# FFN up projection: one 512-column matmul for the high weight half times both activation halves

## The chip, the cores and the metric

The kernel runs on one core of a Trainium2 chip. The metric is the device time of that core for one launch, in microseconds. Before the change it is 1241.15 us, the median of three runs (1241.06 to 1241.66).

## The reference, cut to what matters

The program is one layer of a streaming encoder on 256 tokens of width 2048: token mixers with one combined input projection, a cross-attention, and a gated FFN with a causal depthwise convolution of three taps over the tokens. The change touches the FFN alone:

```python
D_MODEL, SEQ, D_FF, FFN_CONV = 2048, 256, 5632, 3

def conv_ffn(u, w_up, conv_w, conv_b, w_down):
    hdn = causal_dwconv(u @ w_up, conv_w, conv_b)
    g, val = jnp.split(hdn, 2, axis=-1)
    return (jax.nn.silu(g) * val) @ w_down

    h = h + conv_ffn(rmsnorm(h, norm_ffn[l]), ffn_w_up[l], ffn_conv_w[l], ffn_conv_b[l], ffn_w_down[l])
```

Everything is float32, so w_up is 2048 x 11264 and w_down is 5632 x 2048.

## The kernel before, in words

**Precision by halves.** TensorE works on the type float32r here. Each float32 operand is split into a high half (its value in float32r) and a low half (the rest). A product is the sum of three matmuls into the same PSUM columns: high weight by high activation, high weight by low activation, low weight by high activation. `three` (L1243 to L1251) issues them: L1249, L1250 and L1251 with the weight tile as the stationary operand and 256 tokens moving, L1246 to L1248 with the activations stationary and 512 weight columns moving. Each matmul instruction has its own weight load (LDWEIGHTS, on the row of PEld).

**Chunks.** All weights come in chunks of 128 x 2048 (1 MB) through a ring of three slots. SyncE (`load`, L236) fetches chunk n into `raw` when the low half of chunk n-3 is made. ScalarE (`split`, L368 to L374) waits for the landing and for the products of chunk n-3 and copies `raw` to `hi`. VectorE (`split`, L731 to L738) subtracts and writes `lo`, which lets TensorE start on the chunk and SyncE refill `raw`.

**The activations.** They stand in SBUF in transposed form as `uh` (high) and `ul` (low), two tiles of 128 x 16 x 256.

**The FFN.** It is a loop over 11 groups. A group has 12 chunks: 8 of w_up, each of them one tile of 128 hidden features (gate and value tiles in turn, c = 0 to 7), then 4 of w_down (c = 8 to 11). An up tile is `tile_product` (L1253): for each of 16 slices k of the input width, three matmuls of 256 columns into the first 256 columns of bank c % 2, so 48 matmuls. Each of the four down chunks is `row_product` (L1266) with 24 matmuls of 512 columns, 96 in all.

**Around an up tile.** PE may start tile c when its `lo` is ready and when tile c-2 has been read out of the bank (semaphore `fconv_raw`, L1686). VectorE reads it: L1193 multiplies the bank by `hf_scale` (the token's norm factor) into `craw`. ScalarE applies the first tap with the bias (`first_tap`, L685 to L694), VectorE the other two (`filter_rest`, L1168 to L1180, each instruction followed by a wait for its own end: `go`, L727). On each value tile ScalarE applies silu to the gate (L697), VectorE forms the product (L1180), ScalarE makes its high half (L683) and VectorE the low half (`gated_lo`, L1207). The down products of c = 8 and 9 take k = 0 to 2 first (36 matmuls) and then wait for the last low half.

**Order on the engines.** It is written out by hand. ScalarE, per c: split of chunk c+2, then first tap of tile c-1; at c = 8 the first tap of tile 7 and the high half of the last product come ahead of the split. VectorE, per c: `gated_lo` (c = 3, 5, 7, and 8 after the rest of the filter), split of chunk c+2, read-out of tile c, the other two taps of tile c-1; in c = 9 to 11 it adds the down products to the residual (L1111). The first group is special: tile 0 and tile 1 are computed in pieces while the last activations are still being made, and `hf_scale` is copied out of bank 3 (L1159) just ahead of the first read-out.

Of the kernel before, what the change touches and what calls it, by code (L numbers as in the profile page):

```python
# [19 lines left out]
P = 128  # L20
T = 256
# [70 lines left out]
def products(n):  # L92

    extra = {N_U: 3, N_U + 1: 3, N_U + 2: 6, N_U + 3: 1}
    return n + 1 + sum(v for m, v in extra.items() if m <= n)
# [25 lines left out]
def encoder(nc, x, mem, positions, norm_mix, w_in, mla_q_norm, mla_w_uq, mla_kv_norm, mla_w_ukv, mla_out_norm,  # L121
# [4 lines left out]
    with ctx:  # L126
        def sb(name, shape, dt=F32):
            return ctx.enter_context(nc.sbuf_tensor(name, shape, dt))
# [9 lines left out]
        raw = sb("raw", [P, RING, CH])  # L138
        hi = sb("hi", [P, RING, CH], F32R)
        lo = sb("lo", [P, RING, CH], F32R)  # L140
        uh = sb("uh", [P, KD, T], F32R)
        ul = sb("ul", [P, KD, T], F32R)
        ch = sb("ch", [P, 6, T], F32R)
        cl = sb("cl", [P, 6, T], F32R)
        tab = sb("tab", [P, C_ALL])
# [62 lines left out]
        sil, prod = at(12288, T), at(12544, T)  # L208
        gfin = at(13568, D)
        hf_diag, hf_scale = at(12800, TT, P), at(15616, T)  # L210


        s_ss, s_var, s_std, s_r, s_t = 0, 2, 4, 6, 8
# [151 lines left out]
        def _(act):  # L365
# [311 lines left out]
            def ffn_group(i, last=False):  # L677
                def at_turn(v, per):
                    return i * per + v

                def gated_hi(k):
                    act.wait_ge(S("prod_ready").sem, at_turn(k + 1 + 4, 4))
                    a.mark(act.copy(ch[:, k, :], prod[:, :]), S("gated_hi"))  # L683

                def first_tap(c):  # L685

                    s, v, k = c % 4, c % 2, c // 2
                    act.wait_ge(S("fconv_raw").sem, at_turn(c + 3, 8))

                    act.wait_ge(S("prod_ready").sem, at_turn(k + 3, 4))  # L690
                    tile = at_turn(v * FT + k, 4)
                    a.mark(act.activation(cacc[:, s, :], craw[:, s, :], ACT.Identity,  # L692
                                          scale=vecs[:, bass.ds(tile + (V_FW + 2 * 2 * FT), 1)],
                                          bias=vecs[:, bass.ds(tile + V_FB, 1)]), S("fconv_first"))  # L694
                    if v == 1:
                        act.wait_ge(S("fconv_done").sem, at_turn(2 * k + 1, 8))
                        a.mark(act.activation(sil[:, :], cacc[:, s - 1, :], ACT.Silu), S("silu_ready"))  # L697
                    elif k > 0:
                        gated_hi(k - 1)

                for c in range(GROUP):
                    if c == 8:
                        first_tap(7)
                        gated_hi(3)
                    if not (last and c >= GROUP - 2):
                        split(N_FFN + c + 2, i, GROUP)
                    if 0 < c < 8:
                        first_tap(c - 1)
# [14 lines left out]
        def _(dve):  # L723
# [440 lines left out]
            def ffn_group(i, first=False, last=False):  # L1164
                def at_turn(v, per):
                    return i * per + v

                def filter_rest(c):  # L1168

                    s, v, k = c % 4, c % 2, c // 2  # L1170
                    dve.wait_ge(S("fconv_first").sem, at_turn(c + 1, 8))
                    d.settle()
                    for tap in (1, 2):
                        col = at_turn(v * FT + k + (V_FW + (2 - tap) * 2 * FT), 4)
                        go(dve.scalar_tensor_tensor(out=cacc[:, s, tap:T], in0=craw[:, s, 0:T - tap], scalar=vecs[:, bass.ds(col, 1)],  # L1175
                                                    in1=cacc[:, s, tap:T], op0=ALU.mult, op1=ALU.add),
                           S("fconv_done") if tap == 2 else None)
                    if v == 1:
                        dve.wait_ge(S("silu_ready").sem, at_turn(k + 1, 4))
                        go(dve.tensor_tensor(prod[:, :], sil[:, :], cacc[:, s, :], ALU.mult), S("prod_ready"))  # L1180

                for c in range(GROUP):
                    n = N_FFN + c
                    if c == 8:
                        filter_rest(7)
                        gated_lo(3, at_turn)
                    if c in (3, 5, 7):
                        gated_lo((c - 3) // 2, at_turn)
                    if not (last and c >= GROUP - 2) and not (first and c == 0):
                        split(n + 2, i, GROUP)  # L1190
                    if c < 8:
                        dve.wait_ge(S("products_done").sem, at_turn(products(n), GROUP))
                        d.mark(dve.tensor_tensor(craw[:, c % 4, :], bank[c % 2][:, 0:T], hf_scale, ALU.mult), S("fconv_raw"))  # L1193
                    if 0 < c < 8:
                        filter_rest(c - 1)
                    if c >= 9:
                        for cb in ((c - 9,) if c < 11 else (2, 3)):
                            dve.wait_ge(S("products_done").sem, at_turn(products(N_FFN + 8 + cb), GROUP))
                            for t in range(TT):
                                add_bank(FFN_BANKS[cb] + t, t, cb, S("ffn_added"))  # L1200
                            if last:
                                d.settle()
                                for t in range(TT):
                                    cols = slice(cb * 512, (cb + 1) * 512)
                                    d.mark(dve.tensor_tensor(hwork[:, t, cols], hres[:, t, cols], gfin[:, cols], ALU.mult), step)

            def gated_lo(k, at_turn):  # L1207
# [1 line left out]
                d.mark(dve.tensor_tensor(cl[:, k, :], prod[:, :], ch[:, k, :].bitcast(F32), ALU.subtract), S("gated_lo"))  # L1209

            per = {S("lo_ready"): GROUP, S("fconv_done"): 8, S("prod_ready"): 4, S("gated_lo"): 4, S("ffn_added"): 8,
                   S("fconv_raw"): 8, step: 8}
            start = {s: s.n for s in per}
            start[S("prod_ready")], start[S("fconv_raw")] = 4, 2
            for s in per:
# [20 lines left out]
        def _(pe):  # L1236
# [16 lines left out]
            def tile_product(n, b, cols=P, mid=None, lo_signal=None, ks=(0, KD)):  # L1253

                s = n % RING
                for k in range(*ks):
                    if k == KD // 2 and mid:
                        mid()
                    if lo_signal and k % 2 == 0:
                        pe.wait_ge(S(lo_signal).sem, k + 2)  # L1260
                    last = three(bank[b][0:cols, 0:T], hi[:, s, k * P:k * P + cols], lo[:, s, k * P:k * P + cols],
                                 uh[:, k, :], ul[:, k, :], k == 0, k == KD - 1)
                if ks[1] == KD:
                    last.then_inc(done, 1)

            def row_product(n, xh, xl, k0, b0, start, stop, signal=True, ks=range(4), mid=None):  # L1266

# [397 lines left out]
            def ffn_group(i, first=False):  # L1665
                for c in range(8):
                    n = N_FFN + c
                    if first and c == 0:

                        ready(N_FFN)  # L1670
                        pe.wait_ge(S("hf_lo").sem, 8)
                        tile_product(N_FFN, 0, ks=(0, 8))
                        turn_hf(3)
                        pe.wait_ge(S("hf_lo").sem, 12)
                        tile_product(N_FFN, 0, ks=(8, 12))
                        ready(N_FFN + 1)
                        tile_product(N_FFN + 1, 1, ks=(0, 12))
                        pe.wait_ge(S("hf_lo").sem, 16)
                        tile_product(N_FFN, 0, ks=(12, KD))
                        spread_scale("hf", hf_diag, 3)  # L1680
                        tile_product(N_FFN + 1, 1, ks=(12, KD))
                    if first and c < 2:
                        continue
                    ready(n, i, GROUP)

                    pe.wait_ge(S("fconv_raw").sem, i * 8 + (c + 1))  # L1686
                    tile_product(n, c % 2)
                for c in (8, 9):
                    pe.wait_ge(S("gated_lo").sem, i * 4 + 3)
                    ready(N_FFN + c, i, GROUP)  # L1690
                    row_product(N_FFN + c, ch, cl, 0, FFN_BANKS[c - 8], True, False, signal=False, ks=range(3))
                pe.wait_ge(S("gated_lo").sem, i * 4 + 4)
                for c in (8, 9):
                    row_product(N_FFN + c, ch, cl, 0, FFN_BANKS[c - 8], False, True, ks=range(3, 4))
                for c in (10, 11):
                    ready(N_FFN + c, i, GROUP)
                    if c == 11:
                        pe.wait_ge(S("ffn_added").sem, i * 8 + 2)
                    row_product(N_FFN + c, ch, cl, 0, FFN_BANKS[c - 8], True, True)
# [74 lines left out]
```

## Time and profile before

| what | value |
|---|---|
| median of three runs | 1241.15 us |
| span of the profiled execution, first to last instruction | 1237.7 us |
| own time of the profiled execution | not given apart; the span and the 3.45 us up to the median are what is known |
| TensorE busy (matmuls) | 1207.8 us, 98% |
| VectorE busy | 849.8 us, 69% |
| ScalarE busy | 624.7 us, 50% |
| DMA queue of the weights | 216.31 MB, 59.9% of 16 engines |
| FFN, from the first matmul of tile 0 to the last of the last down product | 476.3 to 1224.6 us |

Busy time of matmuls is not a measure of the pace: a matmul of 256 columns shows as 283 ns, yet the next one starts 120 ns later, since they are pipelined. So the pace of TensorE is read from the starts of matmuls in the timeline, or from the length of a stretch that holds a known number of them. PEclk is the granted clock as a share of full speed.

### The profile page before, as it was taken

To read this page: it belongs to the slowest core of one execution; us is meant where nothing else is said; L and a number is where in the kernel's file an instruction comes from. 1 tells how busy PE (TensorE), PEld (TensorE's weight loads), DVE (VectorE), ACT (ScalarE), POOL (GpSimd) and SP (SyncE) were. 2 spreads that over 40 slices of the span, in tenths; PEclk is the share of its full clock that TensorE was granted. 3 is DMA by queue.
4 is the path that set the end of the run, shared out by engine and by line. 5 is a ranking of instruction groups with operands and counts; after the bars stand their busy time and mean duration, and the time that the engine had idled before them with its cause. 6 is when DMAs were issued, how large, how long until landed. Compare 5 with 4: busy or idle time off the path is not lost.

```text
span 1237.7 us, 21481 instructions
## 1 busy us (share of the span) xinstructions
PE 1207.8 (98%) x8428; PEld 1123.8 (91%) x8428; DVE 849.8 (69%) x1155; ACT 624.7 (50%) x778; POOL 0.2 (0%) x4
## 2 busy tenths in 40 slices
PE   6999999999999999999999999999999999999995
PEld 6899999988888979989898999999898989999994
DVE  6754888777376667766767667667667676676675
ACT  5545664475554557445454544454454545454444
POOL 0000000000000000000000000000000000000000
PEclk9999999999899999999999999999999999999998
DMA  9766756432655445676656757575766667575741
GB/s 274 238 160 169 197 142 171 128 104 68 219 189 170 140 153 166 193 200 183 192 171 184 194 163 203 169 208 179 193 192 179 176 188 198 152 203 168 215 156 68
DMA packets 309933, 217.09 MB, mean 175 GB/s; under 512 B 11414, under 2 KB 272254, under 8 KB 309246
## 3 DMA queue, kind: packets, MB, share of 16 engines
q1 hardware_dynamic: 309710, 216.31, 59.9%
q8 instruction: 32, 0.52, 0.2%
q10 hardware_dynamic: 176, 0.14, 0.1%
q14 instruction: 15, 0.12, 0.0%
HBM read 214.33 MB, written 2.10 MB: 175 GB/s over the span
## 4 chain that ended last, share of the span: by engine, by line
PE 92%; ACT 3%; DVE 2%; DMA 1%; SPq 1%; issue 1%; ACTq 0%; DVEq 0%
PE bank L1249 19%; PE bank L1251 19%; PE bank L1250 19%; PE bank L1246 10%; PE bank L1248 10%; PE bank L1247 10%; PE bank L1345 1%; DVE lo L738 1%; ACT hi L374 1%; PE bank L1376 1%; DMA raw<-in_cross_wkv_dram 1%; PE bank L1317 1%; PE bank L1294 1%; PE bank L1303 1%; PE bank L1355 0%
## 5 line engine op out<-in xcount | busy, mean ns | idle before, releaser
L1249 PE MATMUL bank<-uh,hi 128*128 128x256 f32 (+1 forms) x2000 | 569.9, 285 | 3.5 <-DVE lo L738 3.0
L1250 PE MATMUL bank<-ul,hi 128*128 128x256 f32 (+1 forms) x2000 | 566.4, 283 | 0.0
L1251 PE MATMUL bank<-uh,lo 128*128 128x256 f32 (+1 forms) x2000 | 566.3, 283 | 0.0
L738 DVE TENSOR_TENSOR lo<-raw,hi 128x2048 fp32r<-128x2048 f32 x196 | 448.9, 2290 | 168.0 <-ACT hi L374 166.0
L374 ACT CAST hi<-raw 128x2048 fp32r<-128x2048 f32 x196 | 372.7, 1907 | 347.3 <-PE bank L1251 224.9
L1249 PEld LDWEIGHTS bank<-uh,hi 128*128 128x128 f32 (+1 forms) x2000 | 383.5, 192 | 7.8 <-DVE lo L738 3.2
L1250 PEld LDWEIGHTS bank<-ul,hi 128*128 128x128 f32 (+1 forms) x2000 | 383.7, 192 | 0.5
L1251 PEld LDWEIGHTS bank<-uh,lo 128*128 128x128 f32 (+1 forms) x2000 | 383.5, 192 | 0.0
L1246 PE MATMUL bank<-hi,ch 128*128 128x512 f32 x472 | 185.7, 393 | 1.7 <-DVE cl L1134 1.4
L1247 PE MATMUL bank<-lo,ch 128*128 128x512 f32 x472 | 184.4, 391 | 0.0
L1248 PE MATMUL bank<-hi,cl 128*128 128x512 f32 x472 | 184.3, 390 | 0.0
L1246 PEld LDWEIGHTS bank<-hi,ch 128*128 128x128 f32 x472 | 89.4, 189 | 20.3 <-DVE cl L1134 1.8
L1248 PEld LDWEIGHTS bank<-hi,cl 128*128 128x128 f32 x472 | 89.2, 189 | 18.7
L1247 PEld LDWEIGHTS bank<-lo,ch 128*128 128x128 f32 x472 | 89.4, 189 | 17.8
L1175 DVE SCALAR_TENSOR_TENSOR arena<-arena,vecs 128x255 f32<-128x255 f32 (+1 forms) x176 | 85.2, 484 | 24.6 <-DVE arena L1175 2.3
L1193 DVE TENSOR_TENSOR arena<-bank,arena 128x256 f32<-128x256 f32 x88 | 37.3, 424 | 88.3 <-PE bank L1251 88.1
L692 ACT ACTIVATE arena<-arena,vecs 128x256 f32<-128x256 f32 x88 | 52.7, 599 | 40.4 <-DVE arena L1193 40.3
L1111 DVE TENSOR_TENSOR arena<-arena,bank 128x512 f32<-128x512 f32 x96 | 60.7, 681 | 0.9 <-PE bank L1248 0.9
L774 DVE SCALAR_TENSOR_TENSOR ul<-bank,vecs,uh 128x256 fp32r<-128x256 f32 x64 | 26.6, 477 | 16.2 <-ACT uh L404 16.1
L459 ACT COPY arena<-bank 128x256 f32<-128x256 f32 x22 | 8.2, 371 | 57.9 <-PE bank L1251 57.9
L1209 DVE TENSOR_TENSOR cl<-arena,ch 128x256 fp32r<-128x256 f32 x44 | 18.7, 426 | 27.2 <-ACT ch L683 27.2
L404 ACT ACTIVATE uh<-bank,vecs 128x256 fp32r<-128x256 f32 x64 | 25.6, 472 | 19.5 <-PE bank L1303 14.2
(212 smaller groups left out, 780.0 us busy)
## 6 DMA issues: line engine op xcount, KB each, us to landing
raw<-in_ffn_w_up_dram SPq DMA_DIRECT2D x88, 1024.0 KB, 5.8
raw<-in_ffn_w_down_dram SPq DMA_DIRECT2D x44, 1024.0 KB, 5.1
raw<-in_w_in_dram SPq DMA_DIRECT2D x28, 1024.0 KB, 5.7
raw<-in_w_out_dram SPq DMA_DIRECT2D x16, 1024.0 KB, 5.1
raw<-in_cross_wkv_dram SPq DMA_DIRECT2D x7, 1024.0 KB, 9.2
arena<-in_x_dram SPq DMA_DIRECT2D x4, 1024.0 KB, 5.9
raw<-in_cross_wq_dram SPq DMA_DIRECT2D x4, 1024.0 KB, 5.5
raw<-in_cross_wo_dram SPq DMA_DIRECT2D x4, 1024.0 KB, 5.1
```

The lines of the kernel that those rows point to most:

```text
L374: a.mark(act.copy(hi[:, n % RING, :], raw[:, n % RING, :]), S("hi_ready"))
L692: a.mark(act.activation(cacc[:, s, :], craw[:, s, :], ACT.Identity, scale=vecs[:, bass.ds(tile + (V_FW + 2 * 2 * FT), 1)], bias=vecs[:, ba ...
L738: d.mark(dve.tensor_tensor(lo[:, n % RING, :], raw[:, n % RING, :], hi[:, n % RING, :].bitcast(F32), ALU.subtract), S("lo_ready"))
L1111: d.mark(dve.tensor_tensor(hres[:, t, cb * 512:(cb + 1) * 512], hres[:, t, cb * 512:(cb + 1) * 512], bank[b][:, :], ALU.add), signal)
L1175: go(dve.scalar_tensor_tensor(out=cacc[:, s, tap:T], in0=craw[:, s, 0:T - tap], scalar=vecs[:, bass.ds(col, 1)], in1=cacc[:, s, tap:T], op ...
L1193: d.mark(dve.tensor_tensor(craw[:, c % 4, :], bank[c % 2][:, 0:T], hf_scale, ALU.mult), S("fconv_raw"))
L1246: pe.matmul(dst, xh, wh, start=start, stop=False)
L1247: pe.matmul(dst, xh, wl, start=False, stop=False)
L1248: return pe.matmul(dst, xl, wh, start=False, stop=stop)
L1249: pe.matmul(dst, wh, xh, start=start, stop=False)
L1250: pe.matmul(dst, wh, xl, start=False, stop=False)
L1251: return pe.matmul(dst, wl, xh, start=False, stop=stop)
```

## The change

`uh` and `ul` become the two halves of one tile `ux`, so that for each k the high and the low activations stand side by side, 512 columns in a row. A new `wide_product` takes the place of `tile_product` for the up tiles: per k one matmul of 512 columns (high weight by both halves, into the whole bank) and one of 256 columns (low weight by the high half, into the first 256). The two halves of the bank are added when it is read out: ScalarE copies columns 256 to 511 to SBUF (`low_half`, new instruction, with its own semaphore), VectorE adds this to columns 0 to 255, waits for its own end, and multiplies by `hf_scale` from SBUF. The order of ScalarE gets `low_half(c - 1)` ahead of the split of c+2.

```diff
-        uh = sb("uh", [P, KD, T], F32R)
-        ul = sb("ul", [P, KD, T], F32R)
+        ux = sb("ux", [P, KD, 2, T], F32R)
+        uh, ul = ux[:, :, 0, :], ux[:, :, 1, :]
...
+        up_low = at(13056, T)
...
+                def low_half(c):
+
+                    act.wait_ge(S("products_done").sem, at_turn(products(N_FFN + c), GROUP))
+                    a.mark(act.copy(up_low, bank[c % 2][:, T:2 * T]), S("up_low_taken"))
+
                 for c in range(GROUP):
+                    if 0 < c <= 8:
+                        low_half(c - 1)
                     if c == 8:
                         first_tap(7)
                         gated_hi(3)
...
                     if c < 8:
-                        dve.wait_ge(S("products_done").sem, at_turn(products(n), GROUP))
-                        d.mark(dve.tensor_tensor(craw[:, c % 4, :], bank[c % 2][:, 0:T], hf_scale, ALU.mult), S("fconv_raw"))
+                        dve.wait_ge(S("up_low_taken").sem, at_turn(c + 1, 8))
+                        go(dve.tensor_tensor(craw[:, c % 4, :], bank[c % 2][:, 0:T], up_low, ALU.add))
+                        d.mark(dve.tensor_tensor(craw[:, c % 4, :], craw[:, c % 4, :], hf_scale, ALU.mult), S("fconv_raw"))
...
+            def wide_product(n, b, ks=(0, KD)):
+
+                s = n % RING
+                for k in range(*ks):
+                    wh, wl = hi[:, s, k * P:(k + 1) * P], lo[:, s, k * P:(k + 1) * P]
+                    both_ = ux[:, k, :, :].rearrange("p a b -> p (a b)")
+                    if k < KD - 1:
+                        pe.matmul(bank[b][:, :], wh, both_, start=(k == 0), stop=False)
+                        pe.matmul(bank[b][:, 0:T], wl, uh[:, k, :], start=False, stop=False)
+                    else:
+                        pe.matmul(bank[b][:, 0:T], wl, uh[:, k, :], start=False, stop=False)
+                        pe.matmul(bank[b][:, :], wh, both_, start=False, stop=True).then_inc(done, 1)
```

In `ffn_group` of TensorE every `tile_product` of an up tile becomes a `wide_product` with the same slices.

## Rows read from the trace of the kernel before

**Rows 1.** The page: busy time and instructions of each engine.

```profile
PE 1207.8 (98%) x8428; PEld 1123.8 (91%) x8428; DVE 849.8 (69%) x1155; ACT 624.7 (50%) x778; POOL 0.2 (0%) x4
```

**Rows 2.** Who waited for whom, TensorE alone: waited for, us, times, longest.

```profile
PE bank L1249 <- DVE lo L738: 3.0, 1, 3.0
...
PE bank L1249 <- DVE arena L1193: 0.3, 1, 0.3
```

**Rows 3.** Two windows, 96 down and 384 up matmuls: us, busy per engine, PEclk, DMA.

```profile
795.71:817.50 21.79, 21.79 (x99) 18.03 (x97) 15.51 (x17) 10.16 (x8) 0.00 (x0) 1.00 0.63 180
817.50:863.57 46.07, 46.07 (x386) 46.07 (x384) 30.88 (x36) 21.95 (x22) 0.00 (x0) 1.00 0.64 188
```

**Rows 4.** Timeline of TensorE at both changes of width: start us, duration us.

```profile
795.71 0.40 PE L1246 MATMUL bank<-hi,ch 128*128 128x512 f32 x1
795.94 0.40 PE L1247 MATMUL bank<-lo,ch 128*128 128x512 f32 x1
796.18 0.39 PE L1248 MATMUL bank<-hi,cl 128*128 128x512 f32 x1
...
797.10 0.39 PE L1246 MATMUL bank<-hi,ch 128*128 128x512 f32 x1
...
817.27 0.39 PE L1248 MATMUL bank<-hi,cl 128*128 128x512 f32 x1
817.50 0.28 PE L1249 MATMUL bank<-uh,hi 128*128 128x256 f32 x1
817.61 0.28 PE L1250 MATMUL bank<-ul,hi 128*128 128x256 f32 x1
```

**Rows 5.** The page, costliest groups: a ScalarE copy out of a bank, 256 columns.

```profile
L459 ACT COPY arena<-bank 128x256 f32<-128x256 f32 x22 | 8.2, 371 | 57.9 <-PE bank L1251 57.9
```

**Rows 6.** Timeline of VectorE, tiles 2 to 4 of a steady group.

```profile
834.97 0.42 DVE L1193 TENSOR_TENSOR arena<-bank,arena 128x256 f32<-128x256 f32 x1 [1.53 <-PE bank L1251]
835.54 1.11 DVE L1175 SCALAR_TENSOR_TENSOR arena<-arena,vecs 128x255 f32<-128x255 f32 x2
836.77 0.42 DVE L1180 TENSOR_TENSOR arena<-arena 128x256 f32<-128x256 f32 x1
837.77 0.42 DVE L1209 TENSOR_TENSOR cl<-arena,ch 128x256 fp32r<-128x256 f32 x1 [0.57 <-ACT ch L683]
838.12 2.29 DVE L738 TENSOR_TENSOR lo<-raw,hi 128x2048 fp32r<-128x2048 f32 x1
840.73 0.42 DVE L1193 TENSOR_TENSOR arena<-bank,arena 128x256 f32<-128x256 f32 x1 [0.33 <-PE bank L1251]
```

**Rows 7.** Timelines after tile 7 of that group: first down matmul, then VectorE.

```profile
863.57 0.40 PE L1246 MATMUL bank<-hi,ch 128*128 128x512 f32 x1
...
863.77 0.42 DVE L1193 TENSOR_TENSOR arena<-bank,arena 128x256 f32<-128x256 f32 x1 [0.33 <-PE bank L1251]
...
867.89 0.43 DVE L1209 TENSOR_TENSOR cl<-arena,ch 128x256 fp32r<-128x256 f32 x1 [0.54 <-ACT ch L683]
869.64 2.29 DVE L738 TENSOR_TENSOR lo<-raw,hi 128x2048 fp32r<-128x2048 f32 x1 [1.32 <-ACT hi L374]
```

**Rows 8.** Timelines of the first group: VectorE copy and read-out, then tile 2.

```profile
488.41 0.42 DVE L1159 COPY arena<-bank 128x256 f32<-128x256 f32 x1
489.07 0.42 DVE L1193 TENSOR_TENSOR arena<-bank,arena 128x256 f32<-128x256 f32 x1 [0.24 <-DVE arena L1159]
...
489.64 0.36 PE L1249 MATMUL bank<-uh,hi 128*128 128x256 f32 x1 [0.31 <-DVE arena L1193]
```

**Rows 9.** The page, DMA issues: median us from issue to landing.

```profile
raw<-in_ffn_w_up_dram SPq DMA_DIRECT2D x88, 1024.0 KB, 5.8
```

More of the change, by code:

```diff
@@ L1211, in _ @@
             per = {S("lo_ready"): GROUP, S("fconv_done"): 8, S("prod_ready"): 4, S("gated_lo"): 4, S("ffn_added"): 8,
-                   S("fconv_raw"): 8, step: 8}
+                   S("fconv_raw"): 8, step: 16}
             start = {s: s.n for s in per}
@@ L1671, in ffn_group @@
                         pe.wait_ge(S("hf_lo").sem, 8)
-                        tile_product(N_FFN, 0, ks=(0, 8))
+                        wide_product(N_FFN, 0, ks=(0, 8))
                         turn_hf(3)
                         pe.wait_ge(S("hf_lo").sem, 12)
-                        tile_product(N_FFN, 0, ks=(8, 12))
+                        wide_product(N_FFN, 0, ks=(8, 12))
                         ready(N_FFN + 1)
-                        tile_product(N_FFN + 1, 1, ks=(0, 12))
+                        wide_product(N_FFN + 1, 1, ks=(0, 12))
                         pe.wait_ge(S("hf_lo").sem, 16)
-                        tile_product(N_FFN, 0, ks=(12, KD))
+                        wide_product(N_FFN, 0, ks=(12, KD))
                         spread_scale("hf", hf_diag, 3)
-                        tile_product(N_FFN + 1, 1, ks=(12, KD))
+                        wide_product(N_FFN + 1, 1, ks=(12, KD))
                     if first and c < 2:
@@ L1686, in ffn_group @@
                     pe.wait_ge(S("fconv_raw").sem, i * 8 + (c + 1))
-                    tile_product(n, c % 2)
+                    wide_product(n, c % 2)
                 for c in (8, 9):
```

## The prediction, made before the changed kernel was run

> **What bounds the kernel now.** I read the page first: TensorE is busy for 98% of the span, VectorE for 69%, ScalarE for 50% [rows 1]. That share alone can mislead, because matmuls overlap, so I looked next at who made TensorE wait. From the FFN there are two entries at most, 3.0 us once and 0.3 us once [rows 2], and the second of them is in the first group [rows 8]. In the ten groups after that TensorE never waits. So the FFN lasts as long as its matmuls take to issue, and what counts is the distance from one start to the next.
>
> The two windows give that distance. They are cut at starts of matmuls, and the code says how many lie between: 384 matmuls of 256 columns in 46.07 us, 0.1200 us each, and 96 of 512 columns in 21.79 us, 0.2270 us each, both at granted clock 1.00, the 2.4 GHz level [rows 3]. Doubling the columns adds 0.107 us, not 0.120. So a matmul costs 0.107 us per 256 columns and a **fixed part** of about 0.013 us. The timeline shows the settled distance of wide ones a little lower: from 797.10 to 817.27 there are 89 steps, 0.2266 each [rows 4]. The fixed part is then 2 x 0.1200 - 0.2266 = 0.0134 us.
>
> **The change, part by part.**
>
> TensorE. Per slice k three matmuls of 256 columns (0.3600 us) become one of 512 and one of 256. The columns streamed are the same 768; one fixed part goes. I take 0.2266 + 0.1200 = 0.3466 us, a gain of 0.0134 us per k and 0.214 us per tile of 16. No row shows the two widths in strict alternation, so this price needs bounds. The nearest rows are the two changes of width. Coming from 256 columns, the first six steps of 512 take 797.10 - 795.71 = 1.39 us, 0.2317 each and 0.030 us more in all than six settled ones; the first is 0.23 and the second 0.24. Coming from 512, the step after the last wide one is 0.23 and the first narrow one only 0.11 [rows 4]. So a pair could cost from 0.2266 + 0.113 = 0.340 us (0.11 on the row, taken at 0.113 to stay cautious) to 0.2317 + 0.120 = 0.352 us. I take 0.3466: the slow entry and the quick exit would both be met once per k, and they offset each other.
>
> The Trainium skill (TensorE: Matmul & The Clock Gate, section Back-to-back issue gap) has a rule that speaks against the size: the isolated distance at full clock is N / 2.4 ns plus 2.5 ns. By that rule the removed matmul is worth 2.5 ns, 3.5 us over the whole FFN. The rows disagree: 0.120 us for 256 columns is more than ten ns above 106.7 + 2.5, in a stream where each matmul has its own weight load, so the rows decide here.
>
> How many k. There are 11 x 8 = 88 tiles. Tiles 0 and 1 are bounded otherwise: tile 2 starts when VectorE has read tile 0, which hangs on the copy of `hf_scale` [rows 8], so what TensorE saves on two tiles turns into waiting. That leaves 86 x 16 = 1376 slices and 1376 x 0.0134 = **18.4 us gained**.
>
> Read-out. New on ScalarE is a copy of 256 columns from the bank, 0.37 us by its twin [rows 5]. New on VectorE is a second pass of 0.42 us, and the wait for its own end, 0.15 us by the gap between a read-out's end and the next dependent instruction (835.39 to 835.54) [rows 6]. So `craw` is ready some 0.4 + 0.6 = 1.0 us later after the end of a tile. In the steady groups this lies beside TensorE: a bank is needed again only a whole tile later, 5.55 us, and the read-out was done 0.5 us after the tile and will be done at 1.5. The copy stands ahead of the split on ScalarE and delays it by 0.4 us; the delay passes to VectorE's split and then to SyncE's next load. Measured from the tile's end (just ahead of 834.97), VectorE's split in the slow, odd step ended at 5.5 us (838.12 + 2.29 = 840.41) [rows 6]; it will be at 6.5, and TensorE needs it at 11.1. The load behind it lands in a median of 5.8 us [rows 9], so at 12.3, and ScalarE can't take it ahead of 16.6, when its slot's products end. Cover 4 us.
>
> VectorE's own load. The 5.5 us of that step now becomes longer than a tile of 5.55, so the following read-out starts some 0.9 us late. The next, even step has neither product nor low half and takes it back. Added up from the rows with their gaps: two passes of 0.57 each, two taps 1.23 (835.54 to 836.77) and the split 2.29 make 4.66 us for an even step; product, high half and low half add 1.35 (836.77 to 838.12), so 6.01 for an odd one [rows 6]. A pair takes 10.7 us, against 11.1 us for TensorE. Tight, but under.
>
> End of a group. After tile 7 the chain read-out, filter, product, high half, low half ends at 867.89 + 0.43 = 868.32; TensorE wants it after 36 matmuls from 863.57, at 871.8 [rows 7]. It gets 1.0 us later by the two new instructions and up to 0.9 us more by the backlog: 870.2, so 1.6 us are left. The split behind it ends at 871.9 and will end at 873.8; TensorE wants it after 48 matmuls, at 874.5. Cover 0.7 us, the thinnest of all; were it gone, each group would lose the excess, not the gain.
>
> First group. There the read-out is on the path: tile 2 starts at 489.64, straight behind it [rows 8]. The second pass and its wait put 0.42 + 0.15 = 0.57 us, or 0.66 with the 0.24 gap that stands there now, on the end. I take **0.6 us lost**, once. The tail is not touched.
>
> Layout. `ux` keeps each 256-column row contiguous, so the instructions that write `uh` and `ul` and the other stages cost the same: nothing.
>
> Sum: 18.4 - 0.6 = 17.8 us. The profiled span of 1237.7 becomes 1219.9. What lies around the span, 3.45 us to the median of the runs, is untouched, so the median goes from 1241.15 to **1223.4 us**.
>
> **The rivals.**
>
> *Cheaper alternation.* Each narrow matmul behind a wide one keeps the short step of 0.113: 0.340 us a pair, 1376 x 0.020 = 27.5, less 0.6: 1214.3 us. For it speaks the 0.11 at 817.50; against it that it shows once and is gone on the next step. Chance 0.10.
>
> *Dearer alternation.* Each wide one keeps the entry's 0.2317: 0.3517 a pair, 11.4 gained less 0.6: 1230.4; with the second step's 0.236 to 0.240 on every pair it goes up to no gain at all, 1241.7. The first has 0.12, the second 0.05. The page's 2.5 ns, which would give about 1238, sits between these two; the rows above give it no more than their share.
>
> *Slower.* The entry into wide matmuls cost 0.030 us in all [rows 4]. If this is one price per change of width that is merely spread over six starts, and not a price per wide matmul, strict alternation pays it at every k: 0.3466 + 0.030 = 0.3766 us against 0.3600 now, 1376 x 0.0166 = 22.8 us lost, with the 0.6 about 1264.6. The point from which it decides is 0.0134 us per change, under half of what the entry shows in all. Against it: only 0.007 to 0.010 of it falls on any one step, and the exit gives some back. Chance 0.07.
>
> *VectorE becomes the bound.* Its pair of steps would have to take over 11.1 us; the excess then adds up over the three pairs ahead of the last and eats the 0.7 us of cover at the group's end first. At 11.7 us, 9% more than the rows add up to, it is 1.8 us, and each of 11 groups waits 1 us: 1234.4. Chance 0.05.
>
> **How the numbers follow.** The forecast has what is left, 0.61. The range should leave out 2 in 10: from 1213 (cheap alternation in) to 1234 (dear alternation and the VectorE case in); the no-gain and the slower case, 0.12 together, lie outside, with some of the tails. A measurement of this kernel can tell about 0.2%, 2.5 us, from no change. Faster by more than that: 0.61 + 0.10 + 0.12 + 0.05 and part of the no-gain case, 0.90. Same: 0.03. Slower: 0.07.
>
> **What would show it.** Right: in a steady group the up stretch of 256 matmuls lasts 44.4 us instead of 46.07, wide starts are 0.227 and narrow ones 0.120 apart, TensorE's waits in the FFN stay at two or three entries in the first group, and VectorE's busy time rises by 88 x 0.42 = 37 us, ScalarE's by 33 us. Wrong: a wide step of 0.235 or more (dear), a TensorE wait for `craw` or `lo` in each group (VectorE), or a step after a wide one that grows with each k (slower).

## The result, and the profile after

The changed kernel takes 1233.49 us (median of four runs, 1231.91 to 1234.81) against 1241.41 us before (four runs). The ratio is 0.9938, 95% interval 0.9927 to 0.995: **faster by 7.9 us** (0.6%), where 17.8 us were forecast. The time lies just inside the range of 1213 to 1234 us, whose upper part was there for a dear alternation of widths; the gain is under half of the forecast. The profiled execution took 1234.29 us, with a span of 1232.5.

The page of the changed kernel, its first lines, and the one wait of TensorE that lies in the FFN. Its counterpart before is the 0.3 us of [rows 2]; the 3.0 us entry there belongs to a stage ahead of the FFN.

```profile
span 1232.5 us, 18921 instructions
...
PE 1200.0 (97%) x7020; PEld 1049.7 (85%) x7020; DVE 884.7 (72%) x1243; ACT 655.8 (53%) x866; POOL 0.2 (0%) x4
```

```profile
PE bank L1282 <- DVE arena L1202: 0.9, 1, 0.9
```

1408 matmuls are gone, as the code says. TensorE still waits in the FFN once only, for the read-out in the first group. VectorE is busy 34.9 us longer and ScalarE 31.1 us, near the 37 and 33 of the prediction. So no engine took the bound over. The two windows of the same steady group, cut as in [rows 3] (first the 256 matmuls of its eight up tiles, then the 96 of the down chunks; span, busy time of each engine, clock, DMA):

```profile
816.28:861.50 45.22, 45.22 (x257) 39.22 (x256) 32.86 (x43) 24.42 (x29) 0.00 (x0) 1.00 0.65 192
861.50:883.27 21.77, 21.77 (x98) 18.02 (x96) 16.66 (x19) 10.53 (x9) 0.00 (x0) 1.00 0.65 181
```

The down part did not move (21.79 to 21.77). The up part went from 46.07 to 45.22 us, 0.85 us less, where 1.7 were forecast (44.37). Divided by 128 slices, a pair of a wide and a narrow matmul costs **353.3 ns**, not 346.6. The timeline of TensorE shows how (start, duration; "wide" is a matmul of 512 columns, "narrow" one of 256, and a "step" is the distance from one start to the next):

```profile
838.89 0.40 PE L1282 MATMUL bank<-ux,hi 128*128 128x512 f32 x1
839.12 0.28 PE L1283 MATMUL bank<-ux,lo 128*128 128x256 f32 x1
839.23 0.40 PE L1282 MATMUL bank<-ux,hi 128*128 128x512 f32 x1
839.47 0.28 PE L1283 MATMUL bank<-ux,lo 128*128 128x256 f32 x1
839.58 0.40 PE L1282 MATMUL bank<-ux,hi 128*128 128x512 f32 x1
839.83 0.28 PE L1283 MATMUL bank<-ux,lo 128*128 128x256 f32 x1
839.95 0.40 PE L1282 MATMUL bank<-ux,hi 128*128 128x512 f32 x1
```

Three pairs make a cycle that repeats: wide steps of about 0.23, 0.24 and 0.25 us (rounded starts) with narrow ones of 0.11 or 0.12 between; from 838.89 to 839.95 it is 1.06 us for three, 0.3533 each. The narrow ones are a little quick, as at the exit in [rows 4]. The wide ones never settle to 0.2266: they stay as slow as in the entry of [rows 4], or slower. That is the sign that the prediction had named for dear alternation, a wide step of 0.235 or more.

**Where the 5.2 us of the profiled spans come from.** The first matmul of the FFN, before and changed:

```profile
476.26 0.36 PE L1249 MATMUL bank<-uh,hi 128*128 128x256 f32 x1
```

```profile
478.89 0.48 PE L1282 MATMUL bank<-ux,hi 128*128 128x512 f32 x1
```

Ten groups are shorter by 0.87 us each: 8.7. The first group is shorter by 0.7 from tile 2 to its first down matmul. Against this stand 0.4 us in the stretch from tile 0 to tile 2, 2.6 us by which the FFN starts later, and 1.2 us at the very end, behind the last arithmetic (6.67 us from the end of ScalarE's last instruction to the end of the span, 5.44 before). That makes 5.2. The last two are in stages whose arithmetic the change does not touch, and the prediction did not see them.

**From 5.2 us of span to 7.9 us of median.** Wherever a run has both numbers, its time is 1.7 to 1.9 us above its span (1234.29 against 1232.5). So the profiled execution before took about 1239.5 us, an estimate, and was 1.9 us quicker than its median, while that of the changed kernel was 0.8 us slower than its own. The 3.45 us of the prediction were therefore not all around the span; it used them on both sides, so the forecast does not move.

### The profile page after: what moved, and what is told of

Its sections match the earlier page's. It is cut to its first block, busy times and chain, and to the rows that moved or that the text cites. A ratio compares the mean times of both kernels' runs of the same rounds, so it can differ in the third digit from the quotient of the medians.

```text
span 1232.5 us, 18921 instructions
## 1 busy us (share of the span) xinstructions
PE 1200.0 (97%) x7020; PEld 1049.7 (85%) x7020; DVE 884.7 (72%) x1243; ACT 655.8 (53%) x866; POOL 0.2 (0%) x4
## 4 chain that ended last, share of the span: by engine, by line
PE 92%; DVE 3%; ACT 2%; DMA 2%; issue 1%; SPq 0%; ACTq 0%; DVEq 0%
PE bank L1282 25%; PE bank L1283 12%; PE bank L1255 10%; PE bank L1256 10%; PE bank L1257 10%; PE bank L1258 6%; PE bank L1259 6%; PE bank L1260 6%; PE bank L1286 2%; DVE lo L746 1%; PE bank L1367 1%; DMA raw<-in_cross_wkv_dram 1%; ACT hi L375 1%; PE bank L1398 1%; PE bank L1285 1%; DMA arena<-in_mem_dram 1%
## 5 line engine op out<-in xcount | busy, mean ns | idle before, releaser
L1282 PE MATMUL bank<-ux,hi 128*128 128x512 f32 x1320 | 470.1, 399 | 0.9 <-DVE arena L1202 0.9
L1283 PE MATMUL bank<-ux,lo 128*128 128x256 f32 x1320 | 370.7, 281 | 0.0
L1282 PEld LDWEIGHTS bank<-ux,hi 128*128 128x128 f32 x1320 | 248.0, 188 | 58.7 <-issue 1.2
L1283 PEld LDWEIGHTS bank<-ux,lo 128*128 128x128 f32 x1320 | 249.2, 189 | 4.0
L1258 PE MATMUL bank<-ux,hi 128*128 128x256 f32 (+1 forms) x592 | 170.7, 288 | 1.7 <-DVE lo L746 1.7
L1259 PE MATMUL bank<-ux,hi 128*128 128x256 f32 (+1 forms) x592 | 167.5, 283 | 0.0
L1260 PE MATMUL bank<-ux,lo 128*128 128x256 f32 (+1 forms) x592 | 167.4, 283 | 0.0
L705 ACT COPY arena<-bank 128x256 f32<-128x256 f32 x88 | 32.8, 373 | 208.6 <-PE bank L1286 208.6
L1258 PEld LDWEIGHTS bank<-ux,hi 128*128 128x128 f32 (+1 forms) x592 | 112.9, 191 | 5.2 <-issue 2.4
L1259 PEld LDWEIGHTS bank<-ux,hi 128*128 128x128 f32 (+1 forms) x592 | 112.9, 191 | 0.1
L1260 PEld LDWEIGHTS bank<-ux,lo 128*128 128x128 f32 (+1 forms) x592 | 112.8, 191 | 0.0
L1256 PEld LDWEIGHTS bank<-lo,ch 128*128 128x128 f32 x472 | 89.7, 190 | 18.4
```

Source lines behind the costliest of these rows:

```text
L1256: pe.matmul(dst, xh, wl, start=False, stop=False)
L1258: pe.matmul(dst, wh, xh, start=start, stop=False)
L1259: pe.matmul(dst, wh, xl, start=False, stop=False)
L1260: return pe.matmul(dst, wl, xh, start=False, stop=stop)
L1282: pe.matmul(bank[b][:, :], wh, both_, start=(k == 0), stop=False)
L1283: pe.matmul(bank[b][:, 0:T], wl, uh[:, k, :], start=False, stop=False)
```

## The experiments

All times stand against runs of the kernel before on the same chip, whose medians were 1239.0 to 1240.6 us. On one chip its 23 single runs scatter by 4.7 us (1237.55 to 1242.23), while its group in the FFN is 67.86 us in both of its profiles, so differences of a microsecond are read from the stretches of the trace.

### The layout alone

```diff
-        uh = sb("uh", [P, KD, T], F32R)
-        ul = sb("ul", [P, KD, T], F32R)
+        ux = sb("ux", [P, KD, 2, T], F32R)
+        uh, ul = ux[:, :, 0, :], ux[:, :, 1, :]
```

> The kernel before with the high and low activations side by side in one tile, nothing else. The changed kernel reached the FFN 2.6 us later than the kernel before in its profile. If the new layout is the cause: 1243 to 1244 us, and the FFN's first matmul some 2.6 us later than 476.3. If that delay is a scatter of the loads: the time of the kernel before within 0.5 us (1241.4), and a first matmul that differs from run to run.

Measured 1240.73 us, ratio 1.0002 (0.9993 to 1.001); groups of 67.86 us, first FFN matmul at 475.91. The layout shows no cost, and it is not what delays the FFN.

### The read-out alone

```diff
...
+                    elif k < KD - 1:
+                        pe.matmul(bank[b][:, 0:T], wh, uh[:, k, :], start=False, stop=False)
+                        pe.matmul(bank[b][:, T:2 * T], wh, ul[:, k, :], start=False, stop=False)
+                        pe.matmul(bank[b][:, 0:T], wl, uh[:, k, :], start=False, stop=False)
...
```

> The read-out in two parts as in the change, but 14 of 16 slices by three 256-column matmuls as before (only the first and the last slice are wide, so that the whole bank is opened and closed). If the read-out is free beside TensorE but for the first group: 86 tiles gain 2 x 6.7 ns = 1.2 us, first group loses 0.5, so 1240.5 to 1241.5 us. If the new read-out costs TensorE waits in each group: 1243 us or more.

Measured 1237.16 us, ratio 0.998 (0.997 to 0.9989): the read-out in two parts costs TensorE nothing in the steady groups. The up part of a group:

```profile
815.58:861.40 45.82, 45.82 (x370) 45.11 (x368) 32.93 (x43) 24.33 (x29) 0.00 (x0) 1.00 0.64 188
```

With the settled prices it would be 8 x (14 x 0.3600 + 2 x 0.3466) = 45.87 us; it is 0.05 under. The expectation had put the two wide slices of a tile at 353.3 ns each and asked for 1240.5 to 1241.5 us; the gain of about 2.5 us is more than its 0.7. A pair of wide matmuls that meet at the seam of two tiles does not pay what strict alternation does. The seam in the timeline:

```profile
838.26 0.40 PE L1290 MATMUL bank<-ux,hi 128*128 128x512 f32 x1
838.49 0.40 PE L1282 MATMUL bank<-ux,hi 128*128 128x512 f32 x1
838.73 0.28 PE L1283 MATMUL bank<-ux,lo 128*128 128x256 f32 x1
...
839.66 0.28 PE L1286 MATMUL bank<-ux,hi 128*128 128x256 f32 x1
```

The two wide steps take 0.47 us against 0.453 settled, and the eight narrow steps behind them 0.93 against 0.96. Here the narrow ones have room to win back all that the wide ones lost.

### The matmuls alone

ScalarE's `low_half` is gone as well, and the semaphore counts follow.

```diff
...
-                        dve.wait_ge(S("up_low_taken").sem, at_turn(c + 1, 8))
-                        go(dve.tensor_tensor(craw[:, c % 4, :], bank[c % 2][:, 0:T], up_low, ALU.add))
-                        d.mark(dve.tensor_tensor(craw[:, c % 4, :], craw[:, c % 4, :], hf_scale, ALU.mult), S("fconv_raw"))
+                        dve.wait_ge(S("products_done").sem, at_turn(products(n), GROUP))
+                        d.mark(dve.tensor_tensor(craw[:, c % 4, :], bank[c % 2][:, 0:T], hf_scale, ALU.mult), S("fconv_raw"))
...
```

> The matmuls of the change with the one-instruction read-out of before; the high weight by low activation product is left out of the result. If the alternation of widths is what ate the gain (353.3 ns a pair instead of 346.6): 0.5 us under the changed kernel, 1233.0 us, with the same 5.65 us a tile. If the longer read-out ate it: some 1223 to 1225 us.

Measured 1233.1 us, ratio 0.9935 (0.9921 to 0.995), as expected for the alternation, and the up part is that of the changed kernel to the hundredth:

```profile
816.07:861.29 45.22, 45.22 (x258) 39.22 (x256) 30.87 (x36) 21.99 (x22) 0.00 (x0) 1.00 0.65 193
```

VectorE and ScalarE have 2 us less to do here per group, and TensorE is not faster. What ate the gain is in TensorE's own stream.

### One change of width per tile

The matmuls of a tile in another order: 15 wide, 16 narrow, the last wide one (it has to close the bank).

```diff
...
+                    for k in some:
+                        if k < KD - 1:
+                            wide_one(k)
+                    for k in some:
+                        pe.matmul(bank[b][:, 0:T], lo[:, s, k * P:(k + 1) * P], uh[:, k, :], start=False, stop=False)
+                    if KD - 1 in some:
+                        wide_one(KD - 1).then_inc(done, 1)
```

> The change with its matmuls in another order: 15 wide, then 16 narrow, then the last wide one, so one change of width each way per tile instead of 16. If a change of width is what costs (6.7 ns a pair in alternation; entry 0.030 less exit 0.007 us once per tile): 5.57 us a tile against 5.65, 7.2 us under the changed kernel, 1226 us. If the price belongs to each wide matmul or its neighbours whatever the order: as the changed kernel, 1233.5 us.

Measured **1226.33 us**, ratio 0.9883 (0.9869 to 0.9898). The same instructions in another order are 7 us faster than the changed kernel (ratio 0.9938) and than the matmuls alone on the same chip (1233.1 us). The up part:

```profile
813.38:857.89 44.51, 44.51 (x258) 39.35 (x256) 32.76 (x43) 24.45 (x29) 0.00 (x0) 1.00 0.66 194
```

0.71 us less per group than the change. The rival, a price on each wide matmul whatever its neighbours, is out.

### No change of width in 14 of 16 slices

```diff
...
+                    elif k < KD - 1:
+                        pe.matmul(bank[b][:, 0:384], wh, x384, start=False, stop=False)
+                        pe.matmul(bank[b][:, 0:384], wl, x384, start=False, stop=False)
...
```

> A probe of the price alone: in 14 of 16 slices the pair of 512 and 256 columns is replaced by two matmuls of 384 columns, high weight and low weight in turn, the same 768 columns and the same two weight loads but no change of width. It adds the low weight by half of the low activations and leaves out the high weight by the other half of them. If the change of width is the cost: 346.6 ns a pair, 5.56 us a tile, 1226 us. If the turn of high and low weights, or two matmuls per slice as such, is the cost: 353 ns a pair, 5.65 us a tile, 1233 us.

Measured 1225.37 us, ratio 0.987 (0.9852 to 0.9889). Its up part, and its timeline:

```profile
812.66:857.08 44.42, 44.42 (x258) 43.72 (x256) 32.76 (x43) 24.43 (x29) 0.00 (x0) 1.00 0.66 195
```

```profile
836.08 0.33 PE L1287 MATMUL bank<-ux,lo 128*128 128x384 f32 x1
836.26 0.33 PE L1286 MATMUL bank<-ux,hi 128*128 128x384 f32 x1
836.43 0.33 PE L1287 MATMUL bank<-ux,lo 128*128 128x384 f32 x1
836.60 0.33 PE L1286 MATMUL bank<-ux,hi 128*128 128x384 f32 x1
```

Same number of matmuls, same count of columns, same weights in the same turn: 0.173 us a step, 0.347 a pair, what the prediction's 0.3466 says. The first and the last slice of each tile are still a wide and a narrow matmul; in the other 14 the change of width is gone, and the loss with it. So the turn of high and low weights is not the cause. Together with the run above, where the wide matmuls stay and only their order differs, this settles that the frequent change of width costs the time. What inside TensorE makes it so, no run shows.

### Two, four and eight of a width in a row

The order of the experiment above, in blocks.

> The change with two wide, then two narrow matmuls: 8 changes of width each way per tile. If each change costs what the first two steps of the entry show (6 and 10 ns over 226.6) less 7 ns for the exit: 9 ns a change, 5.62 us a tile, about 1230 us. If the price were per slice and not per change: 5.65 us and 1233 us.

> The change with four wide, then four narrow matmuls: 4 changes each way per tile. If each change costs the first four steps of the entry (24 ns over settled) less 7 for the exit: 17 ns a change, 5.61 us a tile, 1229 to 1230 us. If each change costs the 6.7 ns that alternation shows, whatever its length: 5.57 us a tile, 1226 us.

> The change with eight wide, then eight narrow matmuls: two changes of width each way per tile. Price by the full entry and exit, 23 ns a change: 5.546 + 0.046 = 5.59 us a tile. Measured at one change a tile were 16 ns: then 5.578 us, and about 1227.5 us.

Measured 1228.33, 1228.37 and 1227.72 us, ratios 0.9905 (0.989 to 0.992), 0.9898 (0.9881 to 0.9915) and 0.9906 (0.9889 to 0.9923). Their up parts, two, four, eight:

```profile
812.97:857.74 44.77, 44.77 (x257) 39.09 (x256) 32.80 (x43) 24.43 (x29) 0.00 (x0) 1.00 0.66 193
```

```profile
814.87:859.69 44.82, 44.82 (x257) 39.19 (x256) 32.82 (x43) 24.41 (x29) 0.00 (x0) 1.00 0.65 192
```

```profile
812.68:857.35 44.67, 44.67 (x257) 39.33 (x256) 32.80 (x43) 24.51 (x29) 0.00 (x0) 1.00 0.67 194
```

What is lost over 44.37 us, per group: 0.85 us with blocks of one, 0.40 with two, 0.45 with four, 0.30 with eight, 0.14 with sixteen. Divided by the changes of width (120, 64, 32, 16 and 8 each way; 120 and not 128, since the last slice of a tile has its wide matmul behind the narrow one, next to the first of the following tile) a change costs 7, 6, 14, 19 and 18 ns. Per tile the three runs take 5.60, 5.60 and 5.58 us, where their texts had 5.62, 5.61 and 5.58 to 5.59 for a price that depends on the block, so that idea is near but a little dear. A fixed 6.7 ns a change, the other idea for four (5.57), is not what was measured. With equal blocks the price of one change rises from 6 to 7 ns to 14 and more, near what a full entry less a full exit shows ([rows 4]: 0.030 less 0.007 us); strict alternation pays a small price, but most often. The length of the wide block alone does not set it: the read-out alone has a wide block of two too, between 44 narrow ones, and its change costs nothing (0.05 us under the settled sum, over 8 changes).

### The changed kernel and the kernel before once more

> The changed kernel once more, on the chip of these runs. Its tile should be 5.65 us again and its time 1232 to 1235 us. In its first profile it reached the FFN 2.6 us later than the kernel before; if that is a scatter of the loads it moves by a microsecond or more between this profile and the first, if it belongs to the program it is 2.5 to 3 us again.

> The kernel before once more, for its profile. Its FFN should be the same to the hundredth (67.87 us a group) and its stages ahead of the FFN should scatter. If the 2.6 us by which the changed kernel reached the FFN later are scatter, this profile can lie as late (first FFN matmul near 479); if they belong to the shorter program, it is at 475 to 477.5.

The changed kernel: 1233.67 us, ratio 0.9942 (0.9927 to 0.9957), up part 45.22 us again, first FFN matmul at 478.23. The kernel before: 1240.3 us, ratio 1.0, group 67.86, first FFN matmul at 477.35. The expectations had 2.5 to 3 us again, or a shift of a microsecond or more in the changed kernel; its start moved by 0.7 us and that of the kernel before by 1.1. Between these two profiles the FFN starts 0.9 us later, the end costs 1.2 and the FFN gives 9.1, and the spans differ by just that, 7.0 us (1238.8 and 1231.8). So part of the 2.6 us is scatter of the kernel before. Not all, it seems: put side by side, the profiles of the kernel before and of the two experiments whose TensorE program is about as long start the FFN between 475.1 and 477.4 us, and all nine with the shorter program (16 matmuls and weight loads fewer per up tile) between 477.5 and 479.5.

### A longer program

```diff
...
+            pe.wait_ge(done, products(N_FFN - 1) + GROUP * GROUPS)
+            for r in range(192):
+                pe.matmul(bank[0][0:1, 0:1], ones[:, 0:1], ones[:, 0:1], start=True, stop=True)
```

> The kernel with one change of width per tile, plus 192 tiny matmuls behind the last product, whose result nobody reads; they lie beside the last reads and the final norm of the other engines. Kernels with wide matmuls gained 1 to 2 us less than their groups got shorter, and all reach the FFN later. If a shorter TensorE program is why: this one starts its FFN 1 to 2 us sooner and comes to 1224.5 to 1225.5 us. If it is scatter or something else ahead of the FFN: as without padding, 1226.3 us, or more if the tiny matmuls outlast the tail.

> The changed kernel plus the 192 tiny matmuls behind the last product. All eight kernels with the shorter TensorE program made the low half of chunk 4 some 2.3 to 3.2 us later than the kernel before; all four with a longer one within 0.4 us of it. If the length of the program is why: chunk 4 within 0.5 us of the kernel before again, and the time 1 to 2 us under the changed kernel's 1233.6, near 1232. If the late start is made up elsewhere: chunk 4 early, time as without padding.

> The kernel with one change of width per tile again (15 wide, 16 narrow, 1 wide), beside its padded twin on one chip: ratio 0.988, chunk 4 late by 2.3 to 3.2 us.

> Its padded twin on the same chip. If the program's length costs what its profile showed (2.9 us of span): 1.5 to 3 us under its twin, ratio 0.986. If the ratio of the first comparison holds (0.9883 with and without): within 0.5 us of its twin.

The "chunk 4" of these texts is the fifth full-size `lo` of VectorE, which is chunk 5 in the code. In the kernel before, in the changed one and in the padded kernel with one change of width it reads:

```profile
44.19 2.29 DVE L738 TENSOR_TENSOR lo<-raw,hi 128x2048 fp32r<-128x2048 f32 x1
```

```profile
46.49 2.29 DVE L746 TENSOR_TENSOR lo<-raw,hi 128x2048 fp32r<-128x2048 f32 x1 [1.32 <-ACT hi L375]
```

```profile
43.98 2.29 DVE L746 TENSOR_TENSOR lo<-raw,hi 128x2048 fp32r<-128x2048 f32 x1
```

In the nine profiles with the short program it comes 2.0 to 3.2 us late against 44.19, in the three others that were not padded within 0.4, and in the three padded ones at -0.2, 0.0 and +1.1. Two expectations are missed by this: the changed kernel padded was to lie within 0.5 us, and the second run with one change of width, 2.0 us late, at 2.3 or more. The first FFN matmul of the padded ones is at 475.97, 477.04 and 474.66, where the long programs have it or sooner. The stores of the result at the very end differ too. The issues of DMAs, before, changed and padded (count, size, median us to landing):

```profile
out_dram<-arena SPq DMA_DIRECT2D x8, 256.0 KB, 2.7
```

```profile
out_dram<-arena SPq DMA_DIRECT2D x8, 256.0 KB, 4.0
```

```profile
out_dram<-arena SPq DMA_DIRECT2D x8, 256.0 KB, 3.1
```

2.7 us in all four profiles with the long unpadded program, 3.9 or 4.0 in all nine with the short one, 3.1 in the three padded ones. The last of the eight stores lands 3.3 or 3.4 us after its issue in the long programs and 4.5 or 4.6 in the short ones: that is the 1.2 us at the end. In the padded ones it takes 4.7 to 4.9, and from the end of ScalarE's last instruction to the end of the span it is 6.8 to 7.0 us, no less than the 6.6 or 6.7 of the short ones (5.4 in the long). So the padding brings the start back in these profiles, and the end not. The program's instruction queue moves 32 packets in the four long profiles, 30 in the nine short and 33 in the padded ones; whether that has to do with it is not shown. What can be said is that the kernel pays at both ends for something that goes with its TensorE program and not with the pace of its FFN. In the medians the padding does not show clearly: the first padded kernel takes 1224.58 us, as expected for a gain, but its ratio, 0.9883 (0.9864 to 0.9901), is that of the unpadded one on another chip; on one chip it is 1224.75 against 1225.62 us for the twins, ratios 0.9881 (0.9863 to 0.99) and 0.9879 (0.9862 to 0.9897), neither the 1.5 to 3 us less of one expectation nor quite the 0.5 of the other; the changed kernel padded 1231.95 us, ratio 0.9934 (0.992 to 0.9948), against 0.9938 and 0.9942 without. That the length is what acts, and through what, stays open; the padding changes other things too, such as what TensorE does during the stores.

## Why the prediction was wrong in size

**What bounds the kernel: right.** TensorE's steps set the FFN before and after; the single waits of the first group are all there is.

**The fixed part of a matmul: right.** 0.0134 us per matmul, read from two widths, gives 0.3466 us for a pair; uniform steps of 384 columns cost 0.173 us, so 0.347.

**The price of strict alternation: wrong, and this term of the sum is the step that failed.** "I take 0.3466: the slow entry and the quick exit would both be met once per k, and they offset each other." They don't. A pair costs 0.3533 us: the wide steps stay slow, 0.24 on average by the rounded starts shown above, and what the narrow ones win back, 0.11 to 0.12 instead of 0.12, covers only a part. So 1376 slices gain 1376 x 0.0067 = 9.2 us and not 18.4. The bounds of the prediction, 0.340 and 0.352, were taken from the right rows and too tight by 1 to 2 ns: the upper one stopped at the mean of the entry, 0.2317, though the rows showed a second step of 0.24. The rival "dearer alternation" was the mechanism; the chance of 0.12 for it at 0.3517 and 0.05 above that was far too low for a price that no row showed. The rival "slower", 30 ns at every change, did not come in strict alternation, where a change costs 7 ns; in blocks of four and more it costs 14 to 19.

**The first group: right.** 0.6 us were expected, 0.4 to 0.5 measured: tile 2 starts 1.69 us after the start of the copy of `hf_scale` (492.67 less 490.98), before 1.23 [rows 8]. The rows of the changed kernel:

```profile
490.98 0.42 DVE L1167 COPY arena<-bank 128x256 f32<-128x256 f32 x1
491.64 0.42 DVE L1201 TENSOR_TENSOR arena<-bank,arena 128x256 f32<-128x256 f32 x1 [0.24 <-DVE arena L1167]
492.10 0.43 DVE L1202 TENSOR_TENSOR arena<-arena 128x256 f32<-128x256 f32 x1
```

The second pass follows 0.04 us after the first, not 0.15 as taken from another pair of instructions.

**The cover of the read-out: right.** After tile 7 of the group whose down part starts at 794.51 us, the last low half and the split behind it are:

```profile
799.82 0.43 DVE L1218 TENSOR_TENSOR cl<-arena,ch 128x256 fp32r<-128x256 f32 x1 [0.54 <-ACT ch L684]
801.66 2.29 DVE L746 TENSOR_TENSOR lo<-raw,hi 128x2048 fp32r<-128x2048 f32 x1 [1.41 <-ACT hi L375]
```

They end at 5.7 and 9.4 us after the first down matmul; they are wanted at 8.2 and 10.9. The prediction gave 6.6 and 10.2, so the cover was 1.5 us and not 0.7.

**Ahead of and behind the FFN: not seen.** "The tail is not touched" was true of the code and wrong of the time: the stores at the end land 1.2 us later, and the FFN starts 2.6 us later in one pair of profiles and 0.9 in the other. The FFN itself gives 9.1 us between its first matmul and its last. Less the end that is 7.8 us; less the later start too it is 5.2 and 7.0 in the two profiled pairs; the medians say 7.9 and 6.9. So the alternation explains about 9 of the 10 us that are missing from the forecast, and how much the start took from the median is not resolved within the scatter.

**The Trainium skill's distance** (TensorE: Matmul & The Clock Gate, section Back-to-back issue gap), N / 2.4 ns plus 2.5 ns, was weighed and set aside; that stays right, since settled steps of 384 columns take 173 ns where it has 162.5. It has no term for a change of width, and would have put the gain at an estimated 3.5 us. The alternating pair measures 353.3 ns against an estimate of 325 by the rule.

## What to carry to other kernels

The time saved by merging matmuls is the fixed part of each removed one only if the stream keeps one width; where widths must differ, put all of one width together (here 1226.3 us instead of 1233.5 for the same instructions). A transition that the trace shows once is not a price for a stream made of transitions: its worst step is a safer bound than its mean (single steps here went up to that and a little past it), and the order that avoids the transition is worth a run. When a change shortens an unrolled or looped program, compare the start and the end of the two traces as well, before the gain of the changed stage is booked in full.

## What was not expected of the hardware

- Matmuls of 512 and 256 columns in strict turn, both with their own weight load and at clock 1.00, run in a cycle of three pairs of 1.06 us in all, 6.7 ns a pair over the sum of their settled steps.
- With equal blocks a change of width costs 6 to 19 ns depending on how many of a width stand in a row, and nothing with two wide matmuls between 44 narrow ones; steps of 384 columns with high and low weights in turn cost nothing extra (0.173 us each).
- Stores of 256 KB land in 2.7 us in programs with the long TensorE stream and in 3.9 to 4.0 us in those with the short one, 3.1 with tiny matmuls added behind it.
